# Summing weight quarters by accumulating DMAs instead of on GpSimd, in a two-layer encoder kernel

## What is computed

```python
def swiglu_ffn(x, w_gate_up, w_down):
    g, u = jnp.split(x @ w_gate_up, 2, axis=-1)
    return (jax.nn.silu(g) * u) @ w_down

for layer in range(DEPTH):
    x = x + FFN_RES * swiglu_ffn(rms_norm(x, ffn1_norm[layer]), ...)
    h = rms_norm(x, mix_norm[layer])
    ...
    x = x + FFN_RES * swiglu_ffn(rms_norm(x, ffn2_norm[layer]), ...)
```

## Time and profile before

| | us |
|---|---|
| median of 3 runs | 2021.71 |
| the profiled execution's own time | 2022.85 |
| its span in the trace | 2021.1 |
| TensorE matmul busy | 1796.9 (89%) |
| VectorE busy | 1664.0 (82%) |
| GpSimd busy | 1238.7 (61%) |
| ScalarE busy | 952.1 (47%) |
| mean granted TensorE clock | 0.950 of full |

### The profile page before, as it was taken

How to read it: one execution, slowest core, us unless ns; L and a number is a source line. 1 busy time by engine, 2 the same in 40 slices (tenths; PEclk the granted TensorE clock), 3 DMA queues, 4 the chain that set the end, 5 groups by cost and what they waited for, 6 DMA issues and landing times. The chain is left out here.

```text
span 2021.1 us, 34518 instructions
## 1 busy us (share of the span) xinstructions
PE 1796.9 (89%) x12889; PEld 1670.4 (83%) x12889; DVE 1664.0 (82%) x2324; ACT 952.1 (47%) x1784; POOL 1238.7 (61%) x863
## 2 busy tenths in 40 slices
PE   4988989999969899899688998999999788898997
PEld 4988979977868898798588988997867588898995
DVE  6799899867678899986778989867796678989997
ACT  4444444546544444444444454444465454444442
POOL 1788798701139978876298788760000178879771
PEclk6999999999989899999898999999999888999999
DMA  3323323343223232333133232334212132332321
GB/s 106 84 84 84 103 77 94 105 115 85 74 63 84 84 105 85 84 105 95 52 84 84 85 103 70 100 90 121 53 40 78 48 95 83 85 86 83 105 74 73
DMA packets 316675, 172.08 MB, mean 85 GB/s; under 512 B 13345, under 2 KB 311518, under 8 KB 316510
## 3 DMA queue, kind: packets, MB, share of 16 engines
q1 hardware_dynamic: 314944, 168.12, 29.6%
q10 hardware_dynamic: 1566, 1.74, 0.3%
HBM read 163.29 MB, written 2.10 MB: 82 GB/s over the span
## 5 line engine op out<-in xcount | busy, mean ns | idle before, releaser
L1767 PE MATMUL bank<-h_all,w_all 128*128 128x256 f32 x2464 | 734.7, 298 | 171.6 <-ACT work L965 95.1
L1768 PE MATMUL bank<-h_all,w_all 128*128 128x256 f32 x2464 | 722.6, 293 | 0.0
L1769 PE MATMUL bank<-h_all,w_all 128*128 128x256 f32 x2464 | 721.8, 293 | 0.0
L1767 PEld LDWEIGHTS bank<-h_all,w_all 128*128 128x128 f32 x2464 | 499.7, 203 | 192.7 <-issue 141.7
L1768 PEld LDWEIGHTS bank<-h_all,w_all 128*128 128x128 f32 x2464 | 500.2, 203 | 0.0
L1769 PEld LDWEIGHTS bank<-h_all,w_all 128*128 128x128 f32 x2464 | 498.9, 202 | 0.0
L1181 DVE TENSOR_TENSOR w_all<-work,w_all 128x1024 fp32r<-128x1024 f32 x360 | 454.3, 1278 | 31.1 <-ACT w_all L865 29.4
L1181 DVE TENSOR_TENSOR w_all<-r_all,w_all 128x512 fp32r<-128x512 f32 (+1 forms) x240 | 349.9, 1458 | 96.7 <-ACT w_all L865 94.8
L723 POOL TENSOR_TENSOR work<-r_all 128x512 f32<-128x512 f32 x120 | 185.8, 1548 | 322.7 <-DMA r_all<-ffn_gu 184.5
L865 ACT ACTIVATE w_all<-work 128x1024 fp32r<-128x1024 f32 x360 | 269.0, 767 | 144.5 <-PE bank L1769 133.9
L1767 PE MATMUL bank<-y_all,w_all 128*128 128x256 f32 x896 | 258.3, 288 | 22.3 <-DVE w_all L1181 17.8
(11 more groups left out here) (186 smaller groups left out, 2865.5 us busy)
## 6 DMA issues: line engine op xcount, KB each, us to landing
r_all<-ffn_gu SPq DMA_DIRECT2D x176, 512.0 KB, 5.2
r_all<-ffn_d SPq DMA_DIRECT2D x70, 512.0 KB, 5.0
r_all<-ffn_d SPq DMA_DIRECT2D x24, 384.0 KB, 3.6
r_all<-a_in SPq DMA_DIRECT2D x10, 512.0 KB, 4.0
r_all<-a_out SPq DMA_DIRECT2D x8, 512.0 KB, 4.3
r_all<-b_out SPq DMA_DIRECT2D x8, 512.0 KB, 3.8
r_all<-b_in SPq DMA_DIRECT2D x5, 512.0 KB, 3.9
r_all<-b_qup SPq DMA_DIRECT2D x16, 144.0 KB, 2.3
```

Source lines behind the costliest of these rows:

```text
L1767: t.matmul(o, wh, xh, start=c == 0 and not on, stop=False, skip_group_check=on)
L1768: t.matmul(o, wh, xl, start=False, stop=False, skip_group_check=on)
L1769: last = t.matmul(o, wl, xh, start=False, stop=c == PAIRED - 1, skip_group_check=on)
```

## The change

The weights are rearranged before the launch so that each unit's quarters lie one behind the other in rows (A11, A12, A22, A21 for a partition), 2 KB for each quarter. SyncE loads A11 with A12, and A22, as plain data, and A21 twice: once into a buffer called a chain (four of them) and once into a buffer called a single (three). GpSimd no longer computes sums. It issues DMAs that read a quarter from DRAM and add it to what stands in SBUF. Three steps follow one another in a chain: `link` 0 adds A22 (filled as FU, for product 5), `link` 1 adds A11 (filled as FB, for product 6), `link` 2 adds A12 (filled as FD, for product 3). Each step waits for the low fill of the step before. `join` adds A11 to the single (filled as FE, for product 7). The signs of the quarters are absorbed by negated sums on the token side and by factors of -0.5 in place of 0.5 at some outputs. FB, before one fill of 1024 values, becomes FU and FB of 512 each; FU alternates between two places.

```diff
-            def weight_sum(f, u, i):
...
-                        g.tensor_tensor(dst, a21, a22, ALU.add).then_inc(sum_done, 1)
...
-                        g.tensor_tensor(dst, quarter(w_sum[:, S_1, :]), a11, ALU.subtract).then_inc(sum_done, 1)
...
-                        g.tensor_tensor(dst, a11, a21, ALU.subtract).then_inc(sum_done, 1)
...
-                        g.tensor_tensor(dst, a12, quarter(w_sum[:, S_2, :]), ALU.subtract).then_inc(sum_done, 1)
+            def link(f, u, step):
+
+                if u >= NU:
+                    return
+                g = NU * f + u
+                if step == 0:
+                    pool.wait_ge(chain_in[g % CHAIN], 16 * (g // CHAIN + 1))
+                elif step == 1:
+                    pool.wait_ge(fill_lo, fill_count(f, FU, u))
+                else:
+                    pool.wait_ge(fill_lo, fill_count(f, FB, u))
+                part = ((2, 0, 1)[step])
+                pool.dma_start(chain[g % CHAIN], unit_source(f, u, slice(part * S, (part + 1) * S)), accum_op=ALU.add
+                               ).then_inc(chain_sum[g % CHAIN], 16)
+
+            def join(f, u):
+
+                if u >= NU:
+                    return
+                pool.wait_ge(single_in[u % SINGLE], single_count(f, u, 1))
+                pool.dma_start(single[u % SINGLE], unit_source(f, u, slice(0, S)), accum_op=ALU.add
+                               ).then_inc(single_sum[u % SINGLE], 16)
...
             def ffn(f, m):
-                for i in range(3):
-                    weight_sum(f, 0, i)
+                link(f, 0, 0)
+                join(f, 0)
+                link(f, 1, 0)
+                join(f, 1)
+                link(f, 0, 1)
+                link(f, 0, 2)
                 for u in range(NU + 1):
-                    if u < NU:
-                        weight_sum(f, u, 3)
-                    weight_sum(f, u + 1, 0)
-                    weight_sum(f, u + 1, 1)
+                    link(f, u + 1, 1)
+                    link(f, u + 2, 0)
+                    join(f, u + 2)
                     if u == 0:
                         power(m)
...
-                    weight_sum(f, u + 1, 2)
...
+                    link(f, u + 1, 2)
                     if u > 0 and UNITS[u - 1][0] == "G":
                         normed_gate(f, u - 1, 1, m)
                         normed_silu(f, u - 1, 1)
```

ScalarE's fills wait for the DMAs' semaphores, and two of them change place:

```diff
-                    act.wait_ge(sum_done, sum_count(f, u, {FB: 1, FE: 2, FD: 3}[kind]) + 1)
+                    act.wait_ge(chain_sum[(NU * f + u) % CHAIN], chain_count(f, u, {FU: 1, FB: 2, FD: 3}[kind]))
...
+                    high_fill(f, FU, u + 1)
                     if gate:
                         act.wait_ge(prod_done, product_count(f, 1, u))
...
+                    high_fill(f, FB, u + 1)
                     high_fill(f, FD, u)
-                    high_fill(f, FB, u + 1)
```

SyncE's loads of a unit, which before were two DMAs of 512 KB:

```diff
+                sp.dma_start(chain[g % CHAIN], unit_source(f, u, A_21)).then_inc(chain_in[g % CHAIN], 16)
...
+                sp.dma_start(single[u % SINGLE], unit_source(f, u, A_21)).then_inc(single_in[u % SINGLE], 16)
...
+                sp.dma_start(dst[:, 0:2 * S], unit_source(f, u, slice(0, 2 * S))).then_inc(in_, 16)
+                sp.dma_start(dst[:, 2 * S:3 * S], unit_source(f, u, slice(2 * S, 3 * S))).then_inc(in_, 16)
```

More of the change, by code:

```diff
@@ L181, in loads @@
 def loads():
[L183 to L197, removed]
+    count = [0] * SLOTS
+    block = {}
+    for n in range(len(BLOCKS)):
+        count[slot(n)] += 1
+        block[n] = 16 * count[slot(n)]
+    return block
+BLOCK_LOADS = loads()
 M_A = 4
@@ L348, in build @@
         w_raw = r_all[:, 0:SLOTS, :].rearrange("p s (k m) -> p s k m", m=P)
-        tables = r_all[:, SLOTS:6, :].rearrange("p a b -> p (a b)")[:, 0:3 * S]
+        r_flat = r_all[:, :, :].rearrange("p a b -> p (a b)")
+        tables = r_flat[:, 8 * S:11 * S]
+        plain = [r_flat[:, 3 * i * S:3 * (i + 1) * S] for i in range(3)]
+        single = [r_flat[:, (9 + i) * S:(10 + i) * S] for i in range(SINGLE)]
         def view(at, *shape):
@@ L489, in build, with product_w, fill, unit_source @@
         block = ctx.enter_context(nc.Block())
-        def product_w(q, c, low):
-            i, j = P_W[q]
+        def product_w(q, u, c, low):
+            i, j = (1 + u % 2, 1) if q == 5 else P_W[q]
             at = j * S + c * P
             return w_all[:, i, low, at:at + P]
[L497 to L511, removed]
-            if kind == FA:
[L513 to L523, removed]
+        def fill(f, kind, u):
+            raw = plain[(u + 2) % 3]
+            linked = chain[(NU * f + u) % CHAIN]
+            if kind == FA:
+                return w_all[:, 0, 0, :], w_all[:, 0, 1, :], raw[:, 0:2 * S]
+            i, j, src = {FC: (2, 0, raw[:, 2 * S:3 * S]), FU: (1 + u % 2, 1, linked), FB: (1, 0, linked),
+                         FD: (3, 1, linked), FE: (3, 0, single[u % SINGLE])}[kind]
+            return w_all[:, i, 0, j * S:(j + 1) * S], w_all[:, i, 1, j * S:(j + 1) * S], src
+        def unit_source(f, u, part):
+            k = UNITS[u]
+            if k[0] == "G":
+                return units_gu[f][k[1], :, part]
+            return units_d[f][PAIRED * k[1] + k[2], :, part]
         def hid_half(t, half):
@@ L582, in load_unit @@
                         sp.wait_ge(mq_ready, 2)
[L583 to L599, removed]
+                if f == 0 and u == 0:
+                    load_plain(f, u)
+                    load_x(2)
+                    load_chain(f, u)
+                    load_x(1)
+                    load_single(f, u)
+                    load_x(3)
+                    return
+                load_chain(f, u)
+                load_single(f, u)
+                load_plain(f, u)
             def load(n, src):
                 f, i = segment(n), n - SEG_AT[segment(n)]
[L603 to L610, removed]
+                if i < SLOTS:
+                    for kind, u in (((FC, NU - 2),), ((FC, NU - 2), (FA, NU - 1)), ((FC, NU - 1),), ((FC, NU - 3),))[i]:
+                        sp.wait_ge(fill_lo, fill_count(f, kind, u))
                 else:
```

177 lines of the change are left out of this document (100 added, 77 removed).

## The result

| | before | changed |
|---|---|---|
| median, 4 runs of each side by side | 2020.93 us | 2060.45 us (2053.9 to 2064.07) |
| span of the profiled execution | 2021.1 us | 2058.1 us |
| mean granted TensorE clock | 0.950 | 0.948 |

The ratio is 1.0192, with a 95% interval of [1.0165, 1.0218]: **slower, by 39.5 us**. The forecast was slower by 87. The sign and the range held, the size did not. One of the four executions of the run e8 fell into a slow state (3379 us) and its ratio leaves it out.

What follows compares the result with a forecast made beforehand. GpSimd, late by its own sums, was taken to hold TensorE through ScalarE. 2022.85 + 62 for gate rounds + 24 for FFN starts = 2109, forecast 2110 us, slower, range 1955 to 2310.

Steps and rivals of the forecast that it cites:

- d = 1.2: Cost in us of one accumulating DMA issue on GpSimd, bounded by 0.37 and 1.75; the change gains under 0.96.
- 352 us per us: Slope over all gate rounds: each us of issue cost on GpSimd adds 352 us to the time.
- 7.7 + 4d: The law: a plain gate round closes through GpSimd, ScalarE and VectorE; with combines the mean is 13.5 us, +62 us overall.
- VectorE gains: VectorE's fills, stretched by GpSimd (1.22 us median, 0.67 least), get quicker, but the round doesn't end on them; counted as nothing.
- 2.8 together: In 8 of 22 gate rounds, combine work on ScalarE and VectorE adds 2.8 us, a mean of 1.0.
- 12.8 us for a gate round: Length of a gate round in the kernel before, from 310.7 us for 18 gate and 8 down rounds.
- When sums land: 0.: Link 1's addition lands near 2.9 us, within 5.1 us of cover before FB needs it, so it costs 0.
- rival 2: Transfers are late: an addition lands in 7 us, 1.9 past its cover, +167 us, 2277 in all; chance 0.19.
- rival 1: A cheap issue, nearer SyncE's 0.37 us: faster, 1935 us, gaining wherever an issue is under 0.96; chance 0.24.
- Start of an FFN +24.: Five issues of 1.2 us ahead of the power at each FFN's start: +6 us, four times; bounds 0 and +45.
- At nothing: No cost from FB's split fill, SyncE's extra issues, negated sums on VectorE, or down rounds' four issues (4.8 us in 10.1).
- signs named ahead: Trace signs: issues of 1.2 us, ScalarE's wait over 400, TensorE's copy waits over 95, clock below 0.95, gate rounds 13.5.

Runs made afterwards that it cites:

- e8: The spread: ring of 1,152 in the changed kernel, link 0 and join of the unit after next issued behind the second half's gate product; 2674.86 us, ratio to before 1.3215.
- e5: Changed kernel with ring of 1,152, plus one unused GpSimd power of 1.03 us ahead of the gate product of units 2 and on; 2068.44 us, ratio to before 1.0231.
- e3: Changed kernel with the 480 DMAs on GpSimd copying their quarter instead of adding it, sums left out; 1901.93 us, ratio to before 0.941.
- e1: Changed kernel with the space for GpSimd's DMA descriptors at 1,152 bytes of each partition instead of 1,024; 2008.8 us, ratio to before 0.9936.
- e4: Kernel before with only the layout changed, rows of 2 KB and two DMAs for each half block, sums on GpSimd; 2020.93 us, ratio 0.9993.
- e14: Ring of 1,152, gate product second, links 1 and 2 as copies, one unused GpSimd power ahead of each first gate product; 1956.86 us, ratio to before 0.9677.

## Why the prediction was wrong in size

The cost of an issue, the durations taken from the trace before and the place where the loop closes were wrong, and the full ring was missing. That the sign held is luck: it hangs on the ring.

- **"d = 1.2"**, bounded by 1.03 and 1.29. Measured 0.9, under the 0.96 at which the prediction's own law breaks even. By the slope of 352 us per us this is 106 us too much. The row it was put beside, the power of 1.03 us on 128 x 4 values, is no floor for an issue: a power of 128 x 1 takes 0.55. (For d = 1.0 the law gives 2035, not the 2040 of the text.)
- **"7.7 + 4d", durations of before.** The law took gate product 1.31, SiLU product 1.15 and low fill 0.95 from a trace in which the sums ran beside them, the last with a median that mixes two sizes. In the trace after they are 0.75, 0.74 and 0.69: 1.8 us in each round, 158 us too much. The prediction saw the effect and set it at nothing ("VectorE gains ... but it isn't what the round ends on"), although the low fill and the products are terms of its own loop.
- **The loop closed at the wrong place.** In the law the second SiLU product hands over to the next round. The trace shows link 1 waiting for the low fill of FU, behind copy 7 and FE on ScalarE: 2.93 us after the second gate product ends (161.17 to 164.10), where the law, with the durations just named, has 1.38. From the first gate product to link 2 it is 3.18 against 3.04, since VectorE begins FB's low fill 0.3 us after FB is there. Together this is 1.7 us, 150 us too little. The delay (e5) shows that GpSimd's time is indeed paid in the steady rounds, 35.7 us for 37.
- **"2.8 together"** for a combine, and **"12.8 us for a gate round"** before. With the larger ring a combine adds 3.2 us to a steady round (14.4 between links 1 against 11.2), 13 us too little in 32 rounds. The 12.8 comes from the first 18 gate rounds of one FFN; reckoned the same way, the 84 intervals inside all four take 12.5 before, so that the forecast adds some 24 us too little.
- **"When sums land: 0."** The estimate of 2.9 us was 5.6. Even so the cover held in the steady gate rounds, where fills waited 0.9 us in all. It failed in the stretches with down units, 134.3 of the 149.6 us, and these stretches took only 1.7 us more than before. So rival 2's 167 us did not come; what the landing costs is what the change could have gained there, 25.0 us by the copies (e3), issues included.
- **The full ring**, 52 us, stands in no step and in no rival. It is the reason why the sign came out as forecast: by e1 the change without it is faster, as rival 1 has it for every d under 0.96. The forecast was right in sign for a cause that it didn't have.
- **"Start of an FFN +24."** The first four rounds of the FFNs take 28.4 us more, the stretches between them 13.2 less; net 15. With the larger ring these are 10.2 and 15.7, net -5.5: what there was of the +24 was the ring again, not late loads.
- **At nothing**, rightly: the layout (e4), the down rounds' own length (+1.7 in both stretches together). The six intervals behind them, at nothing too, cost 22.9, of which the ring gives back 15.5.

Of the signs named ahead, these came: ScalarE's wait over 400 us (563.1), TensorE's waits for copies 6 and 7 over 95 (154.3), longer combine rounds (14.4 against 12.1). The clock tells nothing: 0.948 to 0.955 in the four executions, 0.950 before. The issue rows of 1.2 us did not come, and the fills' waits for DMAs did. Net: 106 and 158 too much, 30 too much for the start without the ring; 150, 13 and 24 too little, 52 missing: 2110 - 294 + 187 + 52 = 2055, against 2060. This is a reckoning from the traces; of its terms only the ring was measured by a run of its own, and 5 us is less than the others are good for.

## What to carry to other kernels

When an operation leaves an engine, take the durations of its neighbours from a stretch where it isn't running, and close the loop through every wait of the new instructions before multiplying by the number of rounds. Moving work to DMAs issued by GpSimd frees the engine only as far as the issues are cheap and the descriptor ring is deep enough for those in flight: idle time "issue" ahead of an issue, with the engine behind it waited for, is the sign, and 128 bytes more were worth 52 us here. Put the issue whose result is needed last behind the product that ScalarE is waiting for (1987.93 us with both, faster than either kernel), but count its slack first, as the spread shows. And read in the trace how long an inserted delay really took before dividing by it.

## What the runs showed of the hardware

- GpSimd's next DMA can start 0.56 us after the last, but an addition of 128 rows of 2 KB holds the work behind it 0.9 us, a copy of the same size 0.55.
- An addition takes 144 packets where the copy takes 80, moves 166 GB/s where SyncE's copies in the same trace move 315, and lands in 5.7 us in the median where a copy lands in 3.9. It slows the others too: SyncE's plain copies of 256 KB into the same buffers (`r_all<-ffn_gu`) land in 5.2 us beside additions and in 4.0 beside copies. The Trainium skill, DMA: Bandwidth & Descriptors, section on the anatomy of a DMA on the gpsimd path, fits 2.0 us and bytes over 436 GB/s, 2.6 us for 256 KB; in this traffic both are longer, and only the quickest copy (2.9) comes near.
- The descriptors' memory at 576, 1,024 and 1,152 bytes gave 2282, 2060 and 2009 us for the same instructions, with at most two, three and four additions in flight. A held issue starts 0.25 to 0.33 us after a landing, and the idle time before it shows no releaser but "issue".
- Without GpSimd's sums VectorE's low fill of 128 x 512 from the same buffers takes 0.69 us in the mean instead of 1.17. And the other way: in e14 GpSimd's power on 128 x 1 values, 0.55 us alone, came in 57 of 88 places while VectorE ran a low fill of 128 x 1024 (two inputs in SBUF); each time it ended 0.42 us after that fill, 1.3 us in most.
